# Scores of two neighbouring heads in one step of the last block's attention

## What is computed

```python
def hybrid_mixer(h, w_in, b_merge, conv_w, w_out_conv, w_out_attn, w_o):
    proj = jnp.einsum("bsd,dc->bsc", h, w_in)          # 10240 columns: xc bg cg zc q k v za g_conv g_attn
    c = causal_depthwise_conv(cg * xc, conv_w)
    y_conv = jnp.einsum("bsc,cd->bsd", jax.nn.silu(zc) * bg * c, w_out_conv)
    o = mixture_of_dilations(q, k, v, alibi_slopes(N_HEADS))
    y_attn = jnp.einsum("bsc,cd->bsd", jax.nn.silu(za) * o, w_out_attn)
    merged = sigmoid(g_conv + b_conv) * y_conv + sigmoid(g_attn + b_attn) * y_attn
    return jnp.einsum("bsd,de->bse", merged, w_o)

# one window of one head
s = jnp.einsum("bnqrhe,bnkrhe->bnrhqk", qs, kb)        # scores, with an ALiBi bias and a mask
p = jnp.exp(s - max(s)); den = sum(p); o = p @ v / den
```

## Time and profile before

| | |
|---|---|
| median of 3 runs | 1389.88 us (1389.69 to 1390.41) |
| the profiled execution | 1390.04 us |
| its span in the profile | 1388.1 us |
| PE busy | 1366.6 us, 98% |
| POOL busy | 1135.2 us, 82% |
| ACT busy, DVE busy | 660.7 us, 454.8 us |
| moved by DMA | 246.95 MB, mean 178 GB/s |

### The profile page before, as it was taken

One profiled execution on the slowest core, in us unless ns is written; L12 is line 12 of the kernel. 1 busy time (PEld: TensorE's weight loads), 2 busy tenths in 40 slices (PEclk: granted clock), 3 DMA queues, 4 the chain that ended last, 5 costly groups with the idle time before them and its releaser, 6 DMA issues.

```text
span 1388.1 us, 18203 instructions
## 1 busy us (share of the span) xinstructions
PE 1366.6 (98%) x6396; PEld 1119.7 (81%) x6396; DVE 454.8 (33%) x1134; ACT 660.7 (48%) x741; POOL 1135.2 (82%) x912
## 2 busy tenths in 40 slices
PE   6999999999999999999999999999999999999997
PEld 5888888888888888888888778888888877788886
DVE  6101134654000156311002884000156134552224
ACT  5444445546444455544443766444455434544531
POOL 5999977849999967998899449999978976679882
PEclk9999999999999999999999999999999999999999
DMA  7666554526655545665565426656554653446550
GB/s 251 211 209 203 188 199 144 196 92 228 200 193 182 182 167 186 206 211 182 183 194 196 136 70 213 192 189 192 193 167 154 211 173 130 126 148 228 185 178 31
DMA packets 160958, 246.95 MB, mean 178 GB/s; under 512 B 8924, under 2 KB 99844, under 8 KB 160772
## 3 DMA queue, kind: packets, MB, share of 16 engines
q1 hardware_dynamic: 158612, 239.42, 52.8%
q10 hardware_dynamic: 2288, 6.75, 1.4%
HBM read 245.10 MB, written 1.05 MB: 177 GB/s over the span
## 4 chain that ended last, share of the span: by engine, by line
POOL 59%; PE 22%; issue 17%; DMA 1%; ACT 1%; DVE 0%; POOLq 0%; ACTq 0%; SPq 0%; DVEq 0%
POOL w_lo L553 59%; PE acc L1858 5%; PE acc L1861 5%; PE acc L1859 5%; PE gu L2358 1%; PE gu L1858 1%; PE gu L1859 1%; PE gu L1861 1%; PE tb L2367 1%; PE tb L1861 1%; PE tb L1859 1%; PE tb L1858 1%; PE tb L2393 0%; DMA x_res<-in_x 0%; DMA w_raw<-in_w_in 0%
## 5 line engine op out<-in xcount | busy, mean ns | idle before, releaser
L553 POOL TENSOR_TENSOR w_lo<-w_raw,w_hi 128x512 fp32r<-128x512 f32 x896 | 1130.1, 1303 | 226.0 <-ACT w_hi L582 225.9
L582 ACT CAST w_hi<-w_raw 128x2048 fp32r<-128x2048 f32 x225 | 425.3, 1909 | 120.4 <-DMA w_raw<-in_w_ffn_in 32.8
L1858 PE MATMUL gu<-w_hi,xT_hi 128*128 128x512 f32 x832 | 330.6, 397 | 3.9 <-DVE w_lo L1782 2.8
L1859 PE MATMUL gu<-w_lo,xT_hi 128*128 128x512 f32 x832 | 324.4, 390 | 0.0
L1861 PE MATMUL gu<-w_hi,xT_lo 128*128 128x512 f32 x708 | 276.8, 391 | 0.0
L1858 PE MATMUL acc<-w_hi,xT_hi 128*128 128x512 f32 x496 | 198.2, 400 | 0.0
L1859 PE MATMUL acc<-w_lo,xT_hi 128*128 128x512 f32 x496 | 193.2, 390 | 0.0
L1858 PEld LDWEIGHTS gu<-w_hi,xT_hi 128*128 128x128 f32 x832 | 156.8, 188 | 35.7 <-DVE xT_lo L1184 3.2
L1861 PE MATMUL acc<-w_hi,xT_lo 128*128 128x512 f32 x468 | 182.7, 390 | 0.0
L1859 PEld LDWEIGHTS gu<-w_lo,xT_hi 128*128 128x128 f32 x832 | 157.0, 189 | 31.2 <-issue 0.2
L1861 PEld LDWEIGHTS gu<-w_hi,xT_lo 128*128 128x128 f32 x708 | 133.3, 188 | 28.6
(11 more groups left out here) (329 smaller groups left out, 1363.7 us busy)
## 6 DMA issues: line engine op xcount, KB each, us to landing
w_raw<-in_w_ffn_in SPq DMA_DIRECT2D x176, 512.0 KB, 4.7
w_raw<-in_w_ffn_out SPq DMA_DIRECT2D x88, 512.0 KB, 4.1
w_raw<-in_w_in SPq DMA_DIRECT2D x80, 512.0 KB, 4.5
w_raw<-in_mlstm_w_in SPq DMA_DIRECT2D x24, 512.0 KB, 4.6
w_raw<-in_w_ple_gate SPq DMA_DIRECT2D x16, 512.0 KB, 4.2
w_raw<-in_w_kv SPq DMA_DIRECT2D x16, 512.0 KB, 4.3
w_raw<-in_mlstm_w_out SPq DMA_DIRECT2D x8, 512.0 KB, 4.1
w_raw<-in_diff_w_q SPq DMA_DIRECT2D x8, 512.0 KB, 4.2
```

The lines of the kernel that those rows point to most:

```text
L553: ins = pool.tensor_tensor(w_lo[:, slot.spl, cols], w_raw[:, slot.raw, cols], w_hi[:, slot.spl, cols].bitcast(F32), ALU.subtract)
L582: nc.scalar.copy(w_hi[:, slot.spl, :], w_raw[:, slot.raw, :]).then_inc(hi_ready, 1)
L1858: mm(out, xh, wh, start=(half == 0 and k == 0), stop=False)
L1859: mm(out, xh, wl, start=False, stop=False)
```

## The change

PE scores two heads in the even steps and none in the odd ones. For each tile it issues the product of head h on the lower rows into `gu`'s bank 0 and that of head h+1 on the upper rows into bank 1, and signals both after the last. The even step waits for the minima of head h-1, not h-2. DVE, ACT, POOL and SP keep their programs.

```diff
@@ -2346,18 +2346,19 @@
                 def step(k):
 
                     h = k
-                    if h < AH:
+                    if h < AH and h % 2 == 0:
                         if h == 0:
                             pe.wait_ge(h_pl_ready, 8)
                         if h >= 2:
-                            pe.wait_ge(h_negmax, h - 1)
+                            pe.wait_ge(h_negmax, h)
                         if h >= 4:
                             pe.wait_ge(h_o_ready, h - 3)
-                        b = slice(AD * (h % 2), AD * (h % 2) + AD)
                         for t in range(TILES):
-                            ins = mm(gu[:, h % 2, P * t:P * t + P * (t + 1)], h_qT[b, h // 2, tok(t)],
-                                     h_kT[b, h // 2, 0:P * (t + 1)], start=True, stop=True)
-                        ins.then_inc(h_scores, 1)
+                            for a in range(2):
+                                b = slice(AD * a, AD * a + AD)
+                                ins = mm(gu[:, a, P * t:P * t + P * (t + 1)], h_qT[b, h // 2, tok(t)],
+                                         h_kT[b, h // 2, 0:P * (t + 1)], start=True, stop=True)
+                        ins.then_inc(h_scores, 2)
```

## The result

| | before | changed |
|---|---|---|
| median of 5 runs | 1390.11 us | 1382.89 us |
| lowest to highest | 1389.69 to 1391.36 us | 1381.70 to 1383.60 us |
| profiled execution, its span | 1390.04 us, 1388.1 us | 1381.70 us, 1379.8 us |

The ratio is 0.9947, with a 95% interval of 0.9936 to 0.9958: 7.4 us faster, between 5.8 and 8.9. It was predicted as 1382.1 us, in a range of 1381.3 to 1385.0.

A forecast was written before the change was run, and what follows sets the result against it. PE's stream was taken to bound the kernel from this attention to the last projection; 7.94 us removed less 0.1 added is 7.84 us, so 1390.04 us becomes 1382.2, put at 1382.1 us for the median, range 1381.3 to 1385.0.

The forecast's parts named there:

- The price of a score part: PE's attention steps: one head's scores cost 1.00 us (0.94 in step 1); eight odd steps lose 7.94 us.
- The second half at 0.01 us: PE's even steps: the second head's products on the other rows add 0.01 us a pair, 0.1 us for eight.
- POOL follows: POOL's subtractions in the attention: 5.01 us a slot against about 6.5 us, so it keeps pace; waiting shrinks some 8 us.
- DVE and ACT keep their rhythm behind each step: Attention: DVE's step still waits for the same transposes in the same PE steps, so DVE and ACT keep pace.
- 4.76 us at step 6: PE's tighter wait for the previous head's minima: at step 6 they would come with 4.76 us to spare.
- Partial overlap: Rival, even steps: the second half is held up, each pair loses 0.35 us, 2.8 us given back, 1384.8 us; chance 0.06.
- The serial case: Rival, even steps: halves run one after the other, 0.7 us a pair, 5.6 us given back, 1387.6 us; chance 0.05.
- waited for the minima: Slower rival: PE waits in even steps for the head just before; minima 6.5 us later would give 1394 us; chance 0.03.
- take over: Rival: POOL takes over after the attention and gives back a part of the gain, within the range; no chance of its own.

The follow-up runs named there:

- the control: The changed kernel with as many products in the same even steps and banks, but all on the lower 64 rows: 1387.64 us, ratio 0.9983.

## Why the prediction was right

**The price of a score part** held. From steps 5 and 17 of the kernel before, 1.00 us; the even and odd steps of the changed kernel differ by 2.15 less 1.14, 1.01 us. Reading whole steps and not the 0.85 us from scores to transposes made the terms right: by the 0.85 us the sum would have been 6.8. The steps show this, the time doesn't: 6.8 less 0.1 would have given 1383.3 us, which lies in the range too.

**The second half at 0.01 us** held: 2.15 against 2.14 us, and the kernel without it is no faster. The estimate from the Trainium skill, "TensorE: Matmul & The Clock Gate", section "Measured speedup vs the span model" (77% of the ideal with four row tiles, so 1384.3 us here) is not borne out with two: per pair, 0.01 us was lost, not 0.30.

**POOL follows** held. Between the first score and the last unit behind the attention it waited 42.9 us before and 34.9 us now; the difference is the forecast 8 us. The row is from 1110 to 1250 us of the changed kernel. Nothing in the chain after 1100 us is POOL's.

```profile
POOL w_lo L553 <- ACT w_hi L582: 34.9, 14, 5.2
```

**"DVE and ACT keep their rhythm behind each step"** was the one step that failed, by 0.3 us of the sum. I had looked at the wait that the change tightens, `h_negmax`, whose 4.76 us at step 6 were never used (4.77 us in the changed kernel), and not at what POOL's moved and shorter pauses do to DVE. In a pause of POOL, DVE's operations on SBUF ran at their short times. The change took 8 us of pauses away and moved the others, DVE was busy for 5.9 us more in this stretch, and where DVE's queue frees a bank for PE with 1.66 us to spare there came a wait. The sum of the pauses doesn't give DVE's time: with four pairs in the first half and with four in the second POOL waited 39.1 and 39.2 us between 1110 and 1250 us, and DVE was busy for 70.6 and 74.9 us. What counts is which operations a pause meets.

**The sum.** 7.94 less 0.05 (0.006 us in each of eight pairs, from the trace) less 0.30 is 7.6 us; by the medians of the runs it is 7.2, by the ratio 7.4, with 5.8 to 8.9 as its interval. The forecast of 1382.1 us was 0.8 us below the median; 0.3 of it is step 15, and the rest is within the spread of the runs. That the profiled execution came still nearer, 1381.70 us, is luck: 0.7 us of it were gained ahead of the change.

**The rivals.** Partial overlap wanted even steps 0.35 us longer, and they are 0.01 us longer. The serial case came out at 1387.64 us in the control, against 1387.6 as worked out from 0.7 us a pair; a pair took 0.65 us, so a part of that agreement is chance. The two banks in one tensor did not keep the halves apart. PE never waited for the minima, and POOL did not take over.

## What to carry to other kernels

Where 64-row products stand between 128-row ones, the price of one more visit is more than its stream: here 1.00 us for 0.65 us of passes. Put the products of both halves of the rows next to each other, here into different banks. With two products a half their order made no difference, but three 128-row transposes between the halves undid the overlap. One bank for both halves, longer runs of one half and fewer operations between them were not tried. And when an engine that is ahead loses its pauses, look at who shared something with it: the pauses may have been another engine's fast time.

## What the runs showed that I had not expected

Products of the upper rows that stand four passes behind those of the lower rows start with them (0.93 us for all eight in either order, where a strict order of starts would by my estimate have made it 1.36). And a DVE operation with both inputs in SBUF took 0.41 us in a pause of POOL and 1.51 us beside POOL's work, so that a saving on PE made DVE busier by 5.9 us in this attention without one instruction more.
